# Smaller routed tiles in an MoE layer, shared units first, and the next layer's norm made inside the closing sum

## What is computed

```python
def rms_norm(x, g):
    y = x * lax.rsqrt(jnp.mean(x * x, axis=-1, keepdims=True) + NORM_EPS)
    return y * g

def moe_ffn(h, router_w, router_bias, w_gu, w_down, shared_gu, shared_down):
    # 64 experts, TOP_K = 6, D_EXPERT = 384
    scores = jax.nn.sigmoid(h @ router_w)
    _, idx = lax.top_k(scores + router_bias, TOP_K)
    gates = jnp.take_along_axis(scores, idx, axis=-1)
    gates = gates / jnp.sum(gates, axis=-1, keepdims=True) * ROUTED_SCALE
    ...
    # each token's rows go through its six experts, and everything through the shared one
    return routed + swiglu(h, shared_gu, shared_down)

# in reference(), per layer
xl = xl + mod_l[5] * y                       # the closing sum of a layer
hl = modulate(rms_norm(xl, norm1_g[l]), mod_l[0], mod_l[1])   # the opening norm of the next
```

## Time and profile before

| | |
|---|---|
| median of 3 executions | 2782.1 us (2777.4 to 2788.9) |
| the profiled execution | 2787.68 us, its span 2785.5 us |
| granted TensorE clock, mean | 0.941 |
| PE busy | 2377.6 us, 85% |
| DVE, ACT, POOL busy | 742.8, 443.1, 323.0 us |
| moved by DMA | 776.12 MB, mean 279 GB/s |

### The profile page before, as it was taken

One profiled execution on the slowest core, in us unless ns is written; L12 is line 12 of the kernel. 1 busy time (PEld: TensorE's weight loads), 2 busy tenths in 40 slices (PEclk: granted clock), 3 DMA queues, 4 the chain that ended last, 5 costly groups with the idle time before them and its releaser, 6 DMA issues. The chain is left out here.

```text
span 2785.5 us, 38829 instructions
## 1 busy us (share of the span) xinstructions
PE 2377.6 (85%) x16229; PEld 1276.6 (46%) x16229; DVE 742.8 (27%) x1589; ACT 443.1 (16%) x901; POOL 323.0 (12%) x380
## 2 busy tenths in 40 slices
PE   4998999989989998889884898998888788788885
PEld 2457744455444444444431356854443334343332
DVE  1364545353111111111102446464210101111111
ACT  1232343210000000000000132352000000000000
POOL 0005300000111111110100003400111111000000
PEclk8999999999999999999997899999999999999997
DMA  8000088445999999999985310015699999999993
GB/s 304 25 21 32 4 317 312 170 153 179 413 427 415 405 409 393 396 399 380 418 345 215 118 46 17 4 66 207 251 425 427 421 422 421 414 413 411 411 413 127
DMA packets 126595, 776.12 MB, mean 279 GB/s; under 512 B 36760, under 2 KB 45096, under 8 KB 69968
## 3 DMA queue, kind: packets, MB, share of 16 engines
q1 hardware_dynamic: 103376, 735.75, 65.4%
q0 software_dynamic: 23040, 37.82, 3.7%
HBM read 770.98 MB, written 44.44 MB: 293 GB/s over the span
## 5 line engine op out<-in xcount | busy, mean ns | idle before, releaser
L1425 PE MATMUL banks<-arena,htreg 128*64 128x384 f32 (+1 forms) x4288 | 922.4, 522 | 184.7 <-DMA arena<-in_exp_w_gu 177.6
L1425 PEld LDWEIGHTS banks<-arena,htreg 128*64 128x64 f32 (+1 forms) x4288 | 455.0, 156 | 622.8 <-issue 388.8
L1446 PE MATMUL banks<-arena,modreg 128*64 128x512 f32 (+1 forms) x1608 | 433.4, 599 | 23.9 <-issue 19.7
L2166 DVE TENSOR_TENSOR modreg<-modreg,banks 128x384 f32<-128x384 f32 x80 | 44.3, 554 | 1063.1 <-ACT modreg L1728 1059.4
L1446 PEld LDWEIGHTS banks<-arena,modreg 128*64 128x64 f32 (+1 forms) x1608 | 155.4, 148 | 245.5 <-issue 242.0
L2475 POOL DMA_INDIRECT htreg<-h_d,lsg x74 | 76.2, 1029 | 1059.6 <-PE banks L1406 929.7
L988 PE MATMUL banks<-arena,htreg 128*128 128x512 f32 (+3 forms) x480 | 159.7, 492 | 0.0
L2321 DVE COPY modreg<-banks 128x512 f32<-128x512 f32 x74 | 51.2, 692 | 319.7 <-PE banks L1446 319.7
L2481 POOL DMA_INDIRECT y_d<-modreg,lst x74 | 73.4, 992 | 478.3 <-DVE modreg L2321 477.7
L1728 ACT ACTIVATE modreg<-banks 128x384 f32<-128x384 f32 x80 | 39.2, 490 | 562.9 <-PE banks L1425 562.9
L1734 ACT ACTIVATE modreg<-banks 128x384 f32<-128x384 f32 x80 | 39.2, 490 | 517.9 <-PE banks L1437 517.9
(11 more groups left out here) (393 smaller groups left out, 2183.9 us busy)
## 6 DMA issues: line engine op xcount, KB each, us to landing
arena<-in_exp_w_gu SPq DMA_DIRECT2D x256, 1536.0 KB, 23.9
arena<-in_exp_w_down SPq DMA_DIRECT2D x128, 1536.0 KB, 23.4
arena<-in_w_mod SPq DMA_DIRECT2D x32, 1024.0 KB, 10.2
arena<-y_d SPq DMA_DIRECT2D x6, 3072.0 KB, 16.8
modreg<-in_w_mod SPq DMA_DIRECT2D x14, 1024.0 KB, 8.5
modreg<-mod_d SPq DMA_DIRECT2D x20, 512.0 KB
arena<-in_w_in SPq DMA_DIRECT2D x4, 2048.0 KB, 9.4
arena<-in_w_out SPq DMA_DIRECT2D x2, 4096.0 KB, 14.1
```

The lines of the kernel that those rows point to most:

```text
L1425: last = mm(gu_bank(n, half)[rows, 0:DE], src[:, k, rows], up4[q][:, i, DE * half:DE * (half + 1)], start=(k == 0), stop=(k == KD - 1))
L1446: last = mm(ps[4 + half][rows, :], actT[:, k, rows], dn3[q][:, k, 512 * half:512 * half + 512], start=(k == 0), stop=(k == KE - 1))
```

## The change

There are now three kinds of routed units: WHOLE = 4 of 128 slots in both layers, BIG = 12 in which rank u has 96 slots and one of the last 12 ranks the other 32, and 18 pairs of 64 and 64. Layer 0 goes from 40 to 34 routed units, layer 1 stays at 34. A big unit is computed as four tiles of 32 columns, three from the one expert's weights and one from the other's. The address arithmetic follows (three more small DVE operations ahead of the lists, two in `overflow_addresses`). All shared units stand ahead of the routed ones, and `overflow_addresses` is issued in the loop, behind `unit_copied(EARLY + 1)`; ACT waits for it before the first routed output, which is written over its inputs. In `combined`, `finished(i-1)` stands right behind tile i's L1837 and waits there for the modulation rows; SP loads them behind y 1, and the small vectors ahead of w_in.

```diff
-WHOLE = (16, 4)
+WHOLE = (4, 4)
+BIG = (12, 12)
...
-            paired = [(u, (u, u + UNITS[l] - WHOLE[l])) for u in range(WHOLE[l], UNITS[l])]
+            big = range(WHOLE[l], WHOLE[l] + BIG[l])
+            paired = [(u, (u, u + NE - big.stop)) for u in big]
+            paired += [(u, (u, u + UNITS[l] - big.stop)) for u in range(big.stop, UNITS[l])]
...
-            order = [(None, (i,)) for i in range(EARLY)]
-            for i in range(EARLY, NOUT[l]):
-                order += [routed.pop(0), (None, (i,))]
-            return order + routed
+            return [(None, (i,)) for i in range(NOUT[l])] + routed
...
-                    if i == YB - 1 and l + 1 < DEPTH:
+                    if i == 1 and l + 1 < DEPTH:
                         load_mod(l + 1, 0, range(2))
                 if l + 1 < DEPTH:
+                    load_small(l + 1)
                     sp.wait_ge(y_added.sem, y_added.at(l, YB))
                     sp.wait_ge(out_psum.sem, out_psum.at(2 * l + 1, 2 * YB))
                     load_projection(l + 1)
-                    load_small(l + 1)
...
-                def rows_of(n):
-                    return [slice(0, P)] if len(WORK[l][n][1]) == 1 else [slice(0, HALF), slice(HALF, P)]
+                def tiles_of(n, qs):
+                    if len(qs) == 1:
+                        return [(slice(0, P), qs[0])]
+                    if WORK[l][n][0] < WHOLE[l] + BIG[l]:
+                        return [(slice(32 * i, 32 * i + 32), qs[i == 3]) for i in range(4)]
+                    return [(half_rows[j], qs[j]) for j in range(2)]
...
                         r = ROUTED_AT[l].index(n)
+                        if r == 0:
+                            act.wait_ge(addr_ready.sem, addr_ready.at(l, 1))
...
                 def finished(i):
                     u, s = 2 * (l + 1), i // 2
+                    if i == 0:
+                        dve.wait_ge(mod_loaded.sem, mod_loaded.at(u, 4))
...
                     stt(acc[:, t, :], yrow[i % YB][:, BY_PE, :], gate[:, i, BY_PE:TOPK], acc[:, t, :], ALU.mult, ALU.add
                         ).then_inc(y_added.sem, 1)
+                    if i and l + 1 < DEPTH:
+                        finished(i - 1)
...
-                        if i == 0:
-                            dve.wait_ge(mod_loaded.sem, mod_loaded.at(2 * (l + 1), 4))
-                        else:
-                            finished(i - 1)
...
                 gates_made()
-                overflow_addresses()
...
                     if n > EARLY:
                         unit_out(n - 1)
+                    else:
+                        overflow_addresses()
```

More of the change, by code:

```diff
@@ L341, in build @@
         shift_by = carve(stat, 416, NE)
-        keycol, rankcol, dropcol = (carve(stat, 480 + i, 1) for i in range(3))
+        keycol, rankcol, dropcol, latecol = (carve(stat, 480 + i, 1) for i in range(4))
         maxcnt = sb("maxcnt", [1, 8], I32)
@@ L1423, in unit_up @@
                             for half in range(2):
-                                for rows, q in zip(rows_of(n), qs):
+                                for rows, q in tiles_of(n, qs):
                                     last = mm(gu_bank(n, half)[rows, 0:DE], src[:, k, rows], up4[q][:, i, DE * half:DE * (half + 1)],
@@ L2158, in _ @@
                 nt_ = slice(0, n_t)
-                U_, W_ = UNITS[l], WHOLE[l]
+                U_, W_, G_ = UNITS[l], WHOLE[l], BIG[l]
                 lo64 = slice(0, NE)
@@ L2216, in _ @@
                 link(red(rankcol[lo64], row64[lo64], AX, ALU.add))
-                link(ts(dropcol[lo64], rankcol[lo64], float(U_), float(U_ - W_), ALU.is_ge, ALU.mult))
-                link(tt(rankcol[lo64], rankcol[lo64], dropcol[lo64], ALU.subtract))
+                link(ts(dropcol[lo64], rankcol[lo64], float(U_), -float(U_ - W_ - G_), ALU.is_ge, ALU.mult))
+                link(ts(latecol[lo64], rankcol[lo64], float(NE - G_), -float(NE - U_), ALU.is_ge, ALU.mult))
+                link(ts(rankcol[lo64], rankcol[lo64], dropcol[lo64], latecol[lo64], ALU.add, ALU.add))
                 link(ts(unit_hot[lo64, 0:U_], K("experts")[lo64, 0:U_], rankcol[lo64], None, ALU.is_equal))
@@ L2225, in _ @@
                 link(dve.tensor_copy(rank, ps[0][:, 0:NE]))
-                link(ts(shift_by, rank, float(U_), float(HALF), ALU.is_ge, ALU.mult))
-                link(ts(cap, rank, float(W_), float(HALF), ALU.is_lt, ALU.mult))
-                link(ts(cap, cap, float(HALF), None, ALU.add))
-                link(tt(over[:, nt_, :], pos[:, nt_, :], bc(cap, 1, n_t), ALU.is_ge))
-                link(tt(adr[:, nt_, :], pos[:, nt_, :], bc(shift_by, 1, n_t), ALU.add))
+                link(ts(shift_by, rank, float(U_), 2.0, ALU.is_ge, ALU.mult))
+                link(stt(shift_by, rank, float(NE - G_), shift_by, ALU.is_ge, ALU.add))
+                link(ts(cap, rank, float(W_), 1.0, ALU.is_lt, ALU.add))
+                for end in (W_ + G_, NE - G_):
+                    link(stt(cap, rank, float(end), cap, ALU.is_lt, ALU.add))
+                link(stt(over[:, nt_, :], bc(cap, 1, n_t), 32.0, pos[:, nt_, :], ALU.mult, ALU.is_le))
+                link(stt(adr[:, nt_, :], bc(shift_by, 1, n_t), 32.0, pos[:, nt_, :], ALU.mult, ALU.add))
                 link(stt(adr[:, nt_, :], over[:, nt_, :], float(NT * P * 2), adr[:, nt_, :], ALU.mult, ALU.add))
@@ L2267, in overflow_addresses @@
                 def overflow_addresses():
-                    link(ts(base, rank, float(U_), float(HALF * U_ - U_ + W_), ALU.is_ge, ALU.mult))
+                    link(ts(base, rank, float(U_), float(HALF * U_ - U_ + W_ + G_), ALU.is_ge, ALU.mult))
                     link(tt(base, base, rank, ALU.add))
-                    link(tt(cnt, cnt, cap, ALU.subtract))
+                    link(ts(shift_by, rank, float(NE - G_), float(32 * U_ - NE + U_), ALU.is_ge, ALU.mult))
+                    link(tt(base, base, shift_by, ALU.add))
+                    link(stt(cnt, cap, -32.0, cnt, ALU.mult, ALU.add))
                     link(red(cntmax[:, 0:1], cnt, AX, ALU.max))
```

## The result

| | before | changed | ratio |
|---|---|---|---|
| median of 4 executions | 2785.48 us | 2739.03 us | 0.9839 (0.9806 to 0.9872) |
| the profiled execution's span | 2785.5 us | 2737.0 us | |

The account below looks back on a forecast made before the run. The DMA engines were taken to bound the experts' weight streams, with chains of waits outside them. −4.0 − 15.6 − 18.7 = −38.3 us from a median of 2782.1 gave 2743.8 us, range 2726 to 2764.

Parts of the forecast that it names:

- A: Layer 0's front: shared units first and late overflow addresses start the fourth unit earlier and shorten its first half, −4.0 us.
- B: Layer 0's weight stream: 34 routed units for 40 raise the rate from 407 to 416 GB/s, −15.6 us.
- the tail of few busy engines: After layer 0's last weights: shares of 0.31 and 0.26 for nine us hint why the rate would depend on units.
- C: Layer 0's closing sum: reordered DVE work and SP loads bring layer 1's first projection forward, −18.7 us.
- D: Layer 1: 34 units kept, 12 pairs become big units, 0 us, with 3 us either way.
- The sum: Whole kernel: all terms together give −38.3 us, a median of 2743.8 us.
- Stage unchanged: Rival: the 397 GB/s belongs to layer 0's traffic, not its units; −22.7 us, 2759.4; chance 0.15.
- Full rate: Rival: layer 0's early 426 GB/s lasts because PE's spare time frees slots earlier; −54.8 us, 2727.3; chance 0.13.
- Closing sum by half: Rival: in layer 0's closing sum tiles keep taking turns, only the 7.06 us wait goes; −26.7 us, 2755.4; chance 0.06.
- Slower: Rival: a big unit's four 32-column tiles run two and two on PE, 34.0 us a unit, +259 us; chance 0.03.
- The second loop: Rival: a capacity of 32 or 64 overflows, so 256 extra passes run, +2.8 ms; chance 0.01.

Follow-up runs that it names:

- front_only: The kernel before with only the shared units put first and the late overflow addresses; 2779.01 us for 2778.47, ratio 0.9993.
- units_only: The kernel before with only the new units (4 whole, 12 big) and their addresses; 2762.15 us for 2778.47, ratio 0.9932.
- the four and the three profiles named above: Layer 0 up to its y load: 856.5 to 859.5 us in four with old front and units, 832.6 to 837.6 in three with the changed layer 0.
- even_before: The kernel before, 40 units kept, with slots moved by both XORs (64 in odd ranks, 4 times three rank bits); 2725.23 us, ratio 0.979.
- even slots: The changed kernel with slots moved by both XORs (64 in odd ranks, 4 times three rank bits); 2703.41 us for 2778.47, ratio 0.9717.
- after_again: The changed kernel itself run once more on another chip, against the kernel before; 2742.11 us for 2779.99, ratio 0.9851.
- turn_only: The changed kernel with slots moved within 32 alone (XOR 4 times three rank bits); 2740.43 us, ratio 0.9846 to the kernel before.
- swap_by_8: The changed kernel with slot halves traded in units 8 to 15 and 24 to 31 alone; 2729.46 us for 2783.23, ratio 0.98.
- crowding: The changed kernel with layer 1's slots filling partitions 0 to 3, 32 to 35, 4 to 7 first; 2779.61 us for 2781.56, ratio 0.9984.

## Why the prediction was right or wrong

**A**, −4.0: right in its steps. The fourth unit starts 2.5 us earlier against the third (2.4 worked out), its first half gives 1.65 (1.75), the late addresses cost nothing (they end at 645.1, DVE's next work comes at 647.7). In the trace of front_only the stretch is 4.5 us shorter; its times can't tell 4 us from none, so the 4.0 is shown for the fourth unit and only likely for the whole.

**B**, −15.6: sign and rate right, 416 forecast and 417 measured. The size was short in the profiled execution, 20.7; units_only gives 19.0, the second profile of the changed kernel 15.7 (857.4 − 837.6 − 4.1), and the means of the four and the three profiles named above 19.3 (858.2 − 834.8 − 4.1). The step that mis-sized it is the sum over the window from 720 to 1440 alone: 293.0 MB at the measured 417 would be 702.7, or 17.3 us, and the rest lies at the stream's edges, outside that window, and in the scatter of these pieces, 5 us between two profiles of one kernel. The reason that I put first, pairs in place of whole units, was wrong. even_before has the 16 whole units and streams at 427. What I had given as a hint, the tail of few busy engines, pointed the right way, though a tail is left with even slots too (0.67 and 0.42), and so did the Trainium skill's rule beside it: fewer units put fewer rows into the first slots, and where those lie is what the rate follows. That the busiest of 16 engines is behind it is read from the Trainium skill's rule, and the series of packets fit it; the runs show the place of the rows, in both directions, and name no engine.

**C**, −18.7: 18.7 by the pieces. The course was the one worked out: transposes on the heels of sum 1 (1486.66 after a sum that ended at 1486.8), w_in issued while the sums run, the last tile's norm exposed for 7.24 us. A tile took 10.6 and 9.3 us for 9.85 worked out. That the small vectors cost nothing was right only just: they were issued from 1478.7 to 1497.9, 19.2 us where I took 13.0, and w_in followed right behind at 1497.95. It was hidden, since L976 started 19.3 us later. The two runs with half the edit show why the sum had to be taken through the whole chain: 5.9 and 7.5 alone don't add up to it.

**D**, 0: 764.4 and 764.3 us. Same 188 rows by the table's estimate, same time, though 12 pairs had become big units.

**The sum** was 8 us short of the measured 46.5. In the profiled execution, whose span fell by 48.5, 5.1 of the missing 10.2 is B and 4.0 the start of the third unit, which the forecast had no reason to hold; after_again, with a ratio of 0.9851, gives 41 us (32 to 51), and the forecast lies inside. So much of the miss is scatter, and some 3.5 us of it B.

**The rivals.** "Stage unchanged" falls with units_only. "Full rate" was right that 426 could be had for the whole stream and wrong on how: PE's spare time doesn't bring it (417 with plenty of it), even slots do, with little of it (even_before, PE busy 602 of 650). "Closing sum by half" is what either half of the edit does alone. "Slower" falls by the rows of the big unit, 64 records in 5.34 us. The second loop never ran.

**Left open.** Why moves within 32 slots alone (turn_only) bring so little, why swap_by_8 loses nothing in layer 1, why crowding costs twice as much a row as spreading gives, and what the tail with even slots is. A count of the busiest engine over a whole layer is too coarse for these, and no row here names an engine.

## What to carry to other kernels

When the DMA share is 1 and the rate is below the best stretch of the same kernel, look at what shares the engines with the big stream and at how it is placed over the partitions: partly filled gathers that always begin at partition 0 cost this kernel 5% of the stream in layer 0 and 2% in layer 1, and seven small operations that vary the place got it back. Look at single packets, too: here the median did not move, and a few per cent of long ones held most of the loss. A low share behind the stream's last transfer is a weak hint, since the even kernel has a tail as well. And in a chain in which two engines take turns and a third loads for both, cost the edits together, through to what is late next.

## What the runs showed of the hardware

Sixteen DMA engines at shares between 0.98 and 1.01 moved 398, 417 or 427 GB/s of the same weights, by where the 5% of gathered and scattered rows lay. So a share of 1 doesn't mean full use: a weight packet that took 0.80 us in place of 0.46 counts as busy throughout. Before the runs I took 426 for the rate of an undisturbed start; it is what the whole stream reaches. Four 32-column tiles with weights of two experts, changed at each instruction, ran in the time of two 64-column ones (5.34 us for half of gate/up).
